# Loading the experts' row tiles through ScalarE's queue instead of SyncE's

## What is computed

```python
def hier_moe(h, rg_w, rg_b, re_w, re_b, w_gate, w_up, w_down):
    ...
    g_p, g_i = lax.top_k(g_prob, 1)                  # the best of 4 groups
    ...
    e_p, e_i = lax.top_k(e_prob, TOP_K_IN_GROUP)     # the best 2 of its 4 experts
    ...
    hid = jax.nn.silu(jnp.einsum('td,edf->tef', t, w_gate)) * jnp.einsum('td,edf->tef', t, w_up)
    y = jnp.einsum('tef,efd->td', hid * combine[:, :, None], w_down)
```

## Time and profile before

| | before |
|---|---|
| median of three runs | 2195.65 us |
| the profiled execution | 2196.99 us |
| its span | 2194.8 us |
| TensorE busy, matmuls | 2052.9 us (94%) |
| VectorE busy | 943.2 us (43%) |
| ScalarE busy | 492.8 us (22%) |
| GpSimd busy | 135.3 us (6%) |
| mean granted TensorE clock | 0.966 |

### The profile page before, as it was taken

How to read it: one execution, slowest core, us unless ns; L and a number is a source line. 1 busy time by engine, 2 the same in 40 slices (tenths; PEclk the granted TensorE clock), 3 DMA queues, 4 the chain that set the end, 5 groups by cost and what they waited for, 6 DMA issues and landing times.

```text
span 2194.8 us, 23228 instructions
## 1 busy us (share of the span) xinstructions
PE 2052.9 (94%) x9155; PEld 1389.1 (63%) x9155; DVE 943.2 (43%) x1988; ACT 492.8 (22%) x791; POOL 135.3 (6%) x171
## 2 busy tenths in 40 slices
PE   5999999999999997999679999999999999799993
PEld 2787776667677783444248877666676668644441
DVE  1135027666766763111242541476666118511114
ACT  1241113434410011111133410134334000111112
POOL 2000000000000002000350000000000000200001
PEclk8999999999999997999889999999999999799997
DMA  9661112333264337999752111042323421599984
GB/s 360 217 229 46 37 41 86 116 96 107 68 211 144 135 116 288 361 355 356 257 170 66 58 37 39 29 135 75 127 68 100 152 97 65 209 338 357 357 308 163
DMA packets 171675, 360.87 MB, mean 164 GB/s; under 512 B 10577, under 2 KB 123793, under 8 KB 160625
## 3 DMA queue, kind: packets, MB, share of 16 engines
q1 hardware_dynamic: 145808, 269.43, 35.3%
q0 software_dynamic: 18384, 64.63, 8.0%
q10 hardware_dynamic: 7376, 25.33, 2.9%
HBM read 303.46 MB, written 58.52 MB: 165 GB/s over the span
## 4 chain that ended last, share of the span: by engine, by line
PE 81%; DMA 10%; DVE 5%; issue 1%; POOL 1%; SPq 1%; ACT 0%; ACTq 0%; DVEq 0%; POOLq 0%
PE PS L974 77%; DMA ring<-in_expert_w_up_dram 6%; PE PS L978 4%; DMA ar<-in_ada_w_dram 1%; POOL rows L950 1%; DMA mg<-rows 1%; DVE ar L1574 1%; DMA xr<-out_y_dram 1%; DMA br<-rows,posi 1%; PE PS L682 1%; DMA rows<-br,posi 0%; DVE ar L711 0%; DVE xr L721 0%; SPq L813 0%; DVE xr L773 0%
## 5 line engine op out<-in xcount | busy, mean ns | idle before, releaser
L974 PE MATMUL PS<-hT,ring 128*128 128x320 f32 (+1 forms) x2624 | 719.2, 438 | 5.7 <-DVE hT L672 4.1
L974 PEld LDWEIGHTS PS<-hT,ring 128*128 128x128 f32 (+1 forms) x2624 | 486.4, 189 | 214.8 <-issue 10.6
L974 PE MATMUL PS<-ring,mg 128*128 128x512 f32 (+1 forms) x1552 | 557.4, 514 | 22.3 <-DMA ring<-in_expert_w_up_dram 8.5
L974 PEld LDWEIGHTS PS<-ring,mg 128*128 128x128 f32 x1552 | 292.4, 193 | 233.8 <-issue 203.8
L535 DVE SCALAR_TENSOR_TENSOR xr<-ring,cs,xr 128x256 f32<-128x256 f32 x560 | 246.7, 482 | 9.9
L974 PE MATMUL PS<-br,ring 128*128 128x320 f32 x768 | 215.6, 434 | 0.8 <-DVE br L1767 0.8
L974 PEld LDWEIGHTS PS<-br,ring 128*128 128x128 f32 x768 | 145.1, 190 | 64.2 <-issue 4.2
L1372 ACT ACTIVATE xr<-PS 128x256 f32<-128x256 f32 (+1 forms) x108 | 56.0, 524 | 553.3 <-PE PS L974 553.3
L974 PE MATMUL PS<-ring,hT 128*128 128x256 f32 x800 | 177.4, 381 | 1.7 <-DVE ar L1574 1.7
L1574 DVE TENSOR_TENSOR mg<-PS,mg 128x256 f32<-128x256 f32 x38 | 16.1, 424 | 377.1 <-ACT mg L1372 377.1
L974 PEld LDWEIGHTS PS<-ring,hT 128*128 128x128 f32 x800 | 150.5, 190 | 26.3 <-issue 5.5
(11 more groups left out here) (232 smaller groups left out, 1500.3 us busy)
## 6 DMA issues: line engine op xcount, KB each, us to landing
ring<-in_w_in_dram SPq DMA_DIRECT2D x50, 1024.0 KB, 7.8
ring<-in_ada_w_dram SPq DMA_DIRECT2D x40, 1024.0 KB, 5.2
ring<-in_expert_w_gate_dram SPq DMA_DIRECT2D x38, 1024.0 KB, 8.5
ring<-in_expert_w_up_dram SPq DMA_DIRECT2D x38, 1024.0 KB, 10.6
ring<-in_expert_w_down_dram SPq DMA_DIRECT2D x38, 1024.0 KB, 5.4
rows<-br ACTq DMA_DIRECT2D x38, 512.0 KB, 9.0
mg<-rows SPq DMA_DIRECT2D x36, 512.0 KB, 11.4
rows<-const POOLq DMA_DIRECT2D x1, 13824.0 KB, 55.7
```

The source lines that it names most:

```text
L974: return nc.tensor.matmul(out, lhsT, rhs, start=start, stop=stop, skip_group_check=True)
```

## The change

The loads of row tiles, except that of the first (tile 2), leave SyncE's program. ScalarE issues them instead: after the SiLU of tile j it loads the rows of tile j+2 into the buffer of tile j, and then goes on to the evacuation of the down product. The same holds in the loop. No semaphore wait is added. Since the loop's last load can now reach one tile further, `rows` grows from 27 to 28 tiles, and the zeroing with it.

```diff
--- before.py
+++ after.py
@@ -819,9 +819,6 @@
                                  A["expert_w_down"][l, e, :, :].rearrange("(k p) d -> p k d", p=P))\
                         .then_inc(on.landed[at], 16)
 
-                def rows_load(tile, s):
-                    sp.dma_start(xg[s], rows[bass.ds(P * tile, P), :]).then_inc(on.xg_in[s], 16)
-
                 for e in range(DIRECT):
                     for part in range(3):
                         on.wait_filled(sp, on.blocks[on.moe_block + 3 * e + part - RING][1])
@@ -831,13 +828,11 @@
                             down_load(e, e)
                 sp.wait_ge(on.scattered, 16 * 2 * T)
                 on.wait_filled(sp, ("xg", 0))
-                rows_load(DIRECT, 0)
+                sp.dma_start(xg[0], rows[P * DIRECT:P * (DIRECT + 1), :]).then_inc(on.xg_in[0], 16)
                 for e in range(DIRECT, NE):
                     on.wait_filled(sp, ("gu", e - 2))
                     for part in range(2):
                         strip_load(e, e % 2, part)
-                    on.wait_filled(sp, ("xg", e - 1))
-                    rows_load(e + 1, (e + 1) % 2)
                     on.wait_filled(sp, ("dn", e - 2))
                     down_load(e, e % 2)
                 sp.wait_ge(on.route_ready, TILE_LIST)
@@ -850,8 +845,6 @@
                     on.wait_filled(sp, ("gu", s), more)
                     for part in range(2):
                         strip_load(e, s, part)
-                    on.wait_filled(sp, ("xg", s + 1), more)
-                    rows_load(tile + 1, (s + 1) % 2)
                     on.wait_filled(sp, ("dn", s), more)
                     down_load(e, s)
 
@@ -897,7 +890,7 @@
                     pool.wait_ge(const_in, 16)
                     pool.dma_start(y_out, x_in).then_inc(x_copied, 16)
                     pool.dma_start(rows.rearrange("(p n) (k c) -> p (n k) c", p=P, k=4),
-                                   cst("att_mask")[:, 0:2 * P].unsqueeze(1).to_broadcast([P, (TILES + 1) * 4, 2 * P])).then_inc(zeroed, 16)
+                                   cst("att_mask")[:, 0:2 * P].unsqueeze(1).to_broadcast([P, (TILES + 2) * 4, 2 * P])).then_inc(zeroed, 16)
                 else:
                     for t in range(T):
                         x = x3[:, t, :]
@@ -1518,6 +1511,10 @@
                     ps = on.wait_filled(act, ("gu", s), more)
                     f(silu, ps[:, 0:FF], ACT.Silu).then_inc(on.silu_ready, 1)
 
+                def rows_load(tile, s):
+
+                    act.dma_start(xg[s], rows[bass.ds(P * tile, P), :]).then_inc(on.xg_in[s], 16)
+
                 def hidden_moved(s, more):
                     ps = on.wait_filled(act, ("ht", s), more)
                     moved(f(hidT[s % 2], ps[:, 0:2 * P].rearrange("p (f s) -> p f s", f=2), ACT.Copy))
@@ -1538,6 +1535,7 @@
                     if j == 1:
                         act.wait_ge(on.scattered, 16 * 2 * T)
                     if j:
+                        rows_load(j + 2, j % 2)
                         rows_stored(j - 1, 0, (j - 1) // 2, j - 1)
                     hidden_moved(j, 0)
                 pairs = act.value_load(exi[0:1, TILES:TILES + 1], min_val=NE // 2, max_val=TILES // 2 - 1)
@@ -1547,6 +1545,7 @@
                         moved_more = 4 * (i - 1)
                         for s in range(2):
                             silu_of(2 + s, more)
+                            rows_load(2 * i + s + 2, s)
                             rows_stored(1 + s, more, i - 1 + s, 2 * i - 1 + s)
                             hidden_moved(2 + s, more)
                 more = 2 * PER_TILE * (pairs - 1)
@@ -1976,7 +1975,7 @@
         A[name] = nc.dram_tensor(f"out_{name}_dram", shape, F32, kind="ExternalOutput").ap()
     A["mod_rows"] = nc.dram_tensor("mod_rows", (4, 2, D), F32, kind="Internal").ap()
     A["rows_h2"] = nc.dram_tensor("rows_h2", (TOK, D), F32, kind="Internal").ap()
-    A["rows"] = nc.dram_tensor("rows", ((TILES + 1) * P, D), F32, kind="Internal").ap()
+    A["rows"] = nc.dram_tensor("rows", ((TILES + 2) * P, D), F32, kind="Internal").ap()
     return A
 
 def kernel(**inputs):
```

## The result

The changed kernel takes 2207.69 us (median of six runs, 2201.58 to 2208.48) against 2195.57 us of the kernel before (six runs): a ratio of 1.0045, 95% interval 1.0032 to 1.0058. It is slower by 0.45%, some 10 us by the ratio and 12 us by the medians. Measured once more beside the last experiments it was 1.0060 (1.0044 to 1.0076). The profiled execution took 2207.98 us, its span is 2205.8 us, 11.0 us more than before.

The account below looks back on a forecast made before the run. TensorE was taken as the bound, with the expert stages close to both limits, TensorE and transfers. Terms of 0 for issues, cover and byte position, plus about +1 us for overtaking, on 2195.65 gave 2196.5 us; range 2189 to 2208.

Parts of the forecast that it names:

- likeliest case: Whole kernel: no change, 2196.5 us, own range 2192 to 2200, chance 0.50.
- first rival: Last 2.5 us of each `up` strip: the row tile overtakes it, about +9 us, 2205 us; chance 0.27.
- three signs named for the slow side: ScalarE's bytes within the `up` strip's last 2 us, landings of 11.3 us and more, more than 7 waits per layer.
- What bounds the stage: Expert stages: TensorE's waits on `up` strips, 3.9 + 4.6 = 8.5 us or 0.4%, cap any gain by earlier strips.
- The trough: Between a batch's issue and its bytes, transfers nearly stop for nearly 2 us; the row tile before travels at its edge.
- Removed and added issues, 0 us: 17 row-load issues per layer leave SyncE and join ScalarE, hidden in idle time on both: 0 us.
- Row tile late: Expert tiles: landing of 11.4 us or more against 10.8 us in hand costs 20 us, 2216 us; chance 0.05.
- The start of the second queue: ScalarE's row tile beside an `up` strip issued earlier: starts when that strip ends, 0 us, against +0.7 to 1.25 us.
- about +1 us: Allowance for tiles in which the row tile does overtake part of a strip, a tenth of the slower case's cost.
- The loop's end: Where TensorE waits for a strip anyway, overtaking costs 0.7 us once more in full per layer.
- Zeroing, 0 us: Stretch of 84 to 140 us: one more tile of zeros hides in idle time, 0 us; 2.1 us if on the path.
- The rival that was faster: SyncE's queue lands each `up` strip 0.3 us sooner, waits shrink: -5.5 us, 2190 us, or 2187; chance 0.18.

Follow-up runs that it names:

- 8 us kernel: Kernel before with each `down` strip issued one tile later, behind the gate and `up` strips, in tiles 3 to 16 of each layer: 2189.10 us, ratio 0.9961.
- queue at the old place: Kernel before with row tiles 4 to 16 loaded at the same moment as SyncE loaded them, but through ScalarE's queue behind its store: 2216.10 us, ratio 1.0088.
- unrolled-only trace: Kernel before with only row tiles 3 to 16 of each layer loaded by ScalarE behind the SiLU, tiles 17 to 19 staying with SyncE: 2204.33 us, ratio 1.0031.

## Why the prediction was right or wrong

The range (2189 to 2208) held the time by 0.3 us, and the measurement repeated, 2208.47 us, lies just outside it. The likeliest case, no change at 2196.5 us, did not come; the first rival did, and its 2205 us was 3 us short. That the number is held is the width of the range and some luck: the argument for the likeliest case failed, and the rival's sum came close because one of its terms was too large and the other too small. Of the three signs named for the slow side, two were seen (bytes of ScalarE's queue before the strip's end, 9 waits per layer instead of 7); landings of 11.3 us and more were the exception.

*What bounds the stage:* right in its place, too low in its size. The waits on `up` strips are what moved. But the 8.5 us of listed waits were no ceiling: earlier strips gave 8 us in the unrolled part alone and 14 us in all tiles. The trace of the 8 us kernel still has 3.2 and 4.7 us of waits at the loop's end, with products of 8.61 and 9.78 us behind them, so a part of the difference is TensorE's clock; the rest isn't assigned.

*The trough:* right. Without any row loads there the time is the same (0.9997).

*Removed and added issues, 0 us:* right. ScalarE's idle time ahead of the down product's evacuation is 3.92 us after and 3.93 us before.

*Row tile late:* did not happen. Landing took 3.2 to 8.5 us.

*The start of the second queue, "I take 0":* this is the step that failed. Its rule, that the row tile starts when the strip issued before it ends, as the store of the earlier trace rows did, holds in some tiles and not in others. At 946 us the row tile comes behind the strip; at 959 us it takes 30% of the bytes; at the loop's end, and in the kernel with the queue at the old place, it travels along with the strip and both land together. The margin that was left to it, "about +1 us", was too small.

The mean delay in the unrolled part is small: 11.97 and 11.83 us against 11.76 and 11.73, where the rival had +0.7 to 1.25 us. But the batches are not alike. Only some strips land so late that they set the time of the next batch but one, which then follows 11.5 to 11.7 us after the landing. Of the 11 batches of the table these are 8 and 10 in the kernel before, and they land at 11.79 and 11.73 us. In the kernel after they are 6 and 6, nearly every second one, and they land at 12.24 and 11.96 us, while the others land at 11.65 and 11.61. Half of the difference, 0.2 and 0.1 us, is about what a tile has grown by, 0.16 and 0.09 us, or 3.3 us in all in this trace; the other trace of the same kernel has 12.26 and 12.06 us.

In these batches the row tile is issued early: 7.1 to 7.2 us after its batch in 20 of the 24 of both traces, and 7.6 to 8.4 us in the 20 batches whose strip isn't waited for, because there TensorE has just waited for the strip of the batch before, and the SiLU comes later by that wait. So it reaches the strip's last bytes just where the strip is due. Closer batches are not the reason: in the profile of after 10 of these 12 follow the one before by 11.9 to 12.6 us, 9 of the other 10 by 11.4. Still, that the early issue is why these strips are late is argued, not shown; some strips landed as late in the kernel without row loads. The rest, up to the 7 us that the unrolled part costs by the ratio, isn't assigned; a single long wait there, as that of 2.00 us at 876.96 us in the unrolled-only trace with a product of 8.80 us instead of 7.10 behind it, costs almost 4 us.

*The loop's end:* mis-sized. The rival had one term of 0.7 us per layer there. Measured are 3.9 and 2.1 us in the profile of after against that of before, whose waits are short there, and +4 us for the loads of this part alone. Two things were missing. The last strip is issued late, 5.4 us after its batch before the change too (probably by SyncE's way out of the loop, which wasn't tested), so that all of the row tile travels beside it: 1.5 us in the mean of the traces. And the working counted only waits, not what a wait does to TensorE's clock: in layer 1 the product behind it takes 3.0 us more.

*Zeroing, 0 us:* right, 1.0002.

*The rival that was faster:* wrong as a course for this change, but its premise, that strips which come earlier are worth several us, is confirmed by another edit: 8 us in the unrolled part, 14 us in all.

## What to carry to other kernels

A transfer put last in a saturated queue may be free, because it fills the gap in which the next batch is only being issued; moved to another queue it is no longer last, and what it overtakes may be the one transfer that the tensor engine waits for. Before moving a load, ask whose bytes it will travel beside and when that one is due, not how long the issue takes. The better edit was to let the due strips start before the wait of a strip that isn't due (ratio 0.9934); with that slack the placing of the row loads no longer mattered.

## What the runs showed of the hardware

- Whether two queues share seems to depend on what is already under way. A row load issued in ScalarE's queue some 3.5 us before the last strip of the other landed came behind it (0.43 MB of SyncE's queue alone, then 0.41 MB of ScalarE's); one issued 5.0 us before the landing took 0.13 of 0.42 MB in a microsecond before the strip's end; and one issued while all strips of its batch were still to go arrived together with the last of them (13.0 and 13.2 us after their issues).
- A wait of TensorE of 1.38 us left its clock at 1.00. In all the traces 23 waits on `up` strips lasted 1.89 to 4.73 us; 16 of them were followed by products of 8.6 to 10.1 us instead of 7.1 us, and 7 (of 2.04 to 2.96 us, one of them in layer 2 of the kernel after) by one of 7.1 us. So the length of the wait alone does not tell whether the clock falls.
- A single issue on SyncE, otherwise 0.47 us, now and then takes 1.0 to 2.3 us. It is seen in both kernels, and its cause wasn't looked into.
